# Feed-forward up projections with h's two parts side by side, 512 columns per matmul

## The chip, the cores and the metric

One core of a Trainium2 chip runs the whole program. The metric is device time in microseconds (us), the median of several executions. The engines are TensorE (PE, with its weight loads shown apart as PEld), VectorE (DVE), ScalarE (ACT), GpSimd (POOL) and SyncE (SP); the last two only issue transfers here.

## What is computed

A decoder trunk of two layers over a sequence of 256 positions, model width 1024, all in float32. Each layer is a token mixer followed by a feed-forward half; only the latter is touched:

```python
def conv_glu(h, w_up, conv_w, conv_b, w_down):
    up = causal_dwconv(h @ w_up, conv_w, conv_b)
    u, g = up[..., :D_FF], up[..., D_FF:]
    return (jax.nn.gelu(g) * u) @ w_down          # D_FF = 2816
...
h = modulate(rmsnorm(x, ffn_pre_g[l]), sh_f, sc_f)
y = conv_glu(h, ffn_w_up[l], ffn_conv_w[l], ffn_conv_b[l], ffn_w_down[l])
x = x + g_f[:, None, :] * rmsnorm(y, ffn_post_g[l])
```

The depthwise convolution has three taps over the positions. The modulation vectors (sh, sc, g) are rows of `ada_w` times a vector; the kernel works them out on VectorE, a tile of 128 x 1024 at a time, all through the layer.

## The kernel before

Matrix products run in a reduced float32 format, so each operand is split into a high part (rounded, by ScalarE) and the remainder (by VectorE), and each product is made of three matmuls: high weights times the remainder of h, low weights times the high part of h, high times high (`mm3`, line 1589). Weights stream in as blocks of 1 MB (128 partitions x 2048) through a ring of three slots: SyncE loads `raw`, ScalarE writes `w_hi` (lines 543 and 920), VectorE writes `w_lo` (lines 1033 and 1533) and so releases `raw` for the next load; TensorE frees the pair of slots when its product ends (semaphore `blk_used`).

The feed-forward half has 11 pairs. Pair i is an up product for the gate (part 0, `up_proj(2i, 0)`), one for the value (part 1, `up_proj(2i+1, 1)`) and then the down product of the pair before (`down_proj(i - 1)`). An up product makes 2 tiles of 128 features (b) x 256 positions, each a sum over 8 chunks (k) of 3 matmuls with 256 moving columns: 48 matmuls. A down product is 24 matmuls of 512 moving columns. Part 0 lies in PSUM bank 4, part 1 in bank 5, both b side by side; bank 6 takes the two `gate_rows` products near the end of the half.

Behind each up product, ScalarE writes the middle tap with its bias from PSUM to `EF` (`conv`, line 901, two instructions), VectorE adds the other two taps (`conv`, line 1510, four instructions), and its semaphore `up_c` lets TensorE write the bank again. ScalarE then applies the gelu to part 0 (line 908), VectorE multiplies the parts into `tmp` (`hidden`, line 1524), ScalarE rounds them (`hidden_hi`, line 912) and VectorE takes the remainder (`hidden_lo`, line 1528; semaphore `f_lo`), which `down_proj(i)` waits for. Every engine's order is written out by hand: the list in the ScalarE part begins at line 922, that of VectorE at line 1535, that of TensorE at line 2049, and an engine that waits holds up everything behind it.

Between these VectorE does the modulation sums: `ada_sum` (line 1026) and `ffn_sum` (line 1549) reduce one 512 KB tile in `adw`, which has two slots; when one is used up, GpSimd issues the next load into it (line 496), and the sum of that tile waits for its landing. In the head of the half VectorE does sums NT and NT+1, then the first convolution, the split of block NM+3 (pair 1's value weights), sum NT+2, the second convolution, the split of block NM+4 (the first down weights), sum NT+3, `hidden(0)` and `hidden_lo(0)`. Sum NT+2 uses the slot that sum NT leaves, NT+3 the one that NT+1 leaves.

## Time and profile before

| | before |
|---|---|
| time, median of 3 runs | 1001.82 us (1000.3 to 1004.57) |
| the profiled execution | 1004.92 us, its span 1003.3 us |
| PE busy | 974.2 us, 97% |
| PEld busy | 912.4 us, 91% |
| DVE busy | 713.8 us, 71% |
| ACT busy | 525.3 us, 52% |
| granted TensorE clock, mean | 0.979 |
| the chain that ended last | PE 94%, DVE 2%, ACT 2% |

The span reaches from the first to the last instruction of the profiled execution; its time has 1.6 us more around it. In the timeline a duration includes the tail of an instruction that overlaps the next one on the same engine, so the pace of a row of equal instructions is read from the distance between their starts. The feed-forward half of layer 0 lies at 327 to 516 us, that of layer 1 at 809 to 998 us.

### The profile page before, as it was taken

The page shows a single profiled execution, that of the slowest core. Times are in us where ns is not written, and L with a number is a line of the kernel's source. Part 1 is how long each engine was busy: PE and PEld are TensorE (multiplying, and loading weights), DVE is VectorE, ACT ScalarE, POOL GpSimd, SP SyncE. Part 2 cuts the span into 40 slices and gives each one's busy share as a digit, 9 for nine tenths or more (in the row PEclk, how much of TensorE's full clock was granted, in tenths as well). Part 3 has the DMA queues.
Part 4 walks back from the last instruction along what each step waited for, and adds up shares of the span by engine and source line. Part 5 has one row for each costly group of instructions (what it writes and reads, how often), then busy time and mean ns, then how long its engine had stood idle before and what let it go on. Part 6 is the DMA issues. An engine that isn't in the chain of part 4 may idle for free.

```text
span 1003.3 us, 17990 instructions
## 1 busy us (share of the span) xinstructions
PE 974.2 (97%) x7040; PEld 912.4 (91%) x7040; DVE 713.8 (71%) x948; ACT 525.3 (52%) x700; POOL 43.8 (4%) x85
## 2 busy tenths in 40 slices
PE   7999999999999999999989999999999999999997
PEld 7999999999987999999978999899998889999996
DVE  2579865766686888787776876666657688767675
ACT  3435857443456654545564366654344666454554
POOL 0000000000000000000000000000100000000000
PEclk7599999999999999999999999999999999999999
DMA  9876745566464777776734874556746557555541
GB/s 354 282 241 211 255 169 168 171 228 212 147 226 152 252 256 247 244 258 233 269 127 134 282 235 129 187 162 208 242 146 231 189 190 260 183 182 191 173 161 42
DMA packets 134137, 206.34 MB, mean 206 GB/s; under 512 B 6336, under 2 KB 104384, under 8 KB 133952
## 3 DMA queue, kind: packets, MB, share of 16 engines
q1 hardware_dynamic: 122416, 162.07, 49.5%
q0 software_dynamic: 11520, 41.95, 11.5%
q10 hardware_dynamic: 144, 1.51, 0.4%
q8 instruction: 42, 0.69, 0.3%
q14 instruction: 15, 0.12, 0.0%
HBM read 204.46 MB, written 1.05 MB: 205 GB/s over the span
## 4 chain that ended last, share of the span: by engine, by line
PE 94%; DVE 2%; ACT 2%; issue 1%; DMA 0%; DVEq 0%; SPq 0%; ACTq 0%
PE banks L1594 81%; PE banks L1654 2%; PE banks L1610 2%; PE banks L1880 1%; PE banks L1883 1%; PE banks L1618 1%; PE banks L1724 1%; PE banks L1706 1%; DVE x L1123 1%; PE banks L1890 1%; PE banks L1743 1%; ACT h L592 1%; PE banks L1752 0%; PE banks L1769 0%; DVE w_lo L1033 0%
## 5 line engine op out<-in xcount | busy, mean ns | idle before, releaser
L1594 PE MATMUL banks<-h_lo,w_hi 128*128 128x256 f32 x1504 | 430.4, 286 | 3.2 <-DVE h_lo L1094 3.2
L1594 PE MATMUL banks<-h_hi,w_lo 128*128 128x256 f32 x1504 | 425.5, 283 | 0.0
L1594 PE MATMUL banks<-h_hi,w_hi 128*128 128x256 f32 x1504 | 425.5, 283 | 0.0
L1594 PEld LDWEIGHTS banks<-h_lo,w_hi 128*128 128x128 f32 x1504 | 288.4, 192 | 6.7 <-DVE h_lo L1094 4.0
L1594 PEld LDWEIGHTS banks<-h_hi,w_lo 128*128 128x128 f32 x1504 | 288.5, 192 | 2.2 <-issue 1.4
L1594 PEld LDWEIGHTS banks<-h_hi,w_hi 128*128 128x128 f32 x1504 | 288.4, 192 | 0.0
L1033 DVE TENSOR_TENSOR w_lo<-raw,w_hi 128x2048 fp32r<-128x2048 f32 x82 | 187.2, 2290 | 71.6 <-ACT w_hi L543 71.5
L543 ACT ACTIVATE w_hi<-raw 128x2048 fp32r<-128x2048 f32 x82 | 156.0, 1910 | 109.6 <-PE banks L1594 99.7
L1533 DVE TENSOR_TENSOR w_lo<-raw,w_hi 128x2048 fp32r<-128x2048 f32 x56 | 128.0, 2286 | 22.7 <-ACT w_hi L920 22.6
L920 ACT ACTIVATE w_hi<-raw 128x2048 fp32r<-128x2048 f32 x56 | 107.2, 1913 | 43.9 <-PE banks L1594 43.9
L1510 DVE SCALAR_TENSOR_TENSOR EF<-banks,par,EF 128x254 f32<-128x254 f32 (+1 forms) x176 | 76.9, 478 | 51.5 <-ACT EF L901 46.0
L901 ACT ACTIVATE EF<-banks,par 128x256 f32<-128x256 f32 x88 | 44.9, 561 | 106.6 <-PE banks L1594 106.6
L1594 PE MATMUL banks<-w_hi,oa_lo 128*128 128x512 f32 x208 | 81.3, 391 | 0.0
L1594 PE MATMUL banks<-w_lo,oa_hi 128*128 128x512 f32 x208 | 81.2, 390 | 0.0
L1594 PE MATMUL banks<-w_hi,oa_hi 128*128 128x512 f32 x208 | 80.9, 389 | 0.0
L496 POOL DMA_DIRECT2D adw<-in_ada_rows x80 | 42.6, 533 | 800.9 <-DVE adw L1026 598.8
L1026 DVE SCALAR_TENSOR_TENSOR adw<-adw,cbc 128x1024 f32<-128x1024 f32 x58 | 70.3, 1220 | 3.6 <-DMA adw<-in_ada_rows 2.4
L831 ACT ACTIVATE lat<-banks 128x512 f32<-128x512 f32 x24 | 14.2, 591 | 74.7 <-PE banks L1594 74.7
L1594 PEld LDWEIGHTS banks<-w_hi,oa_hi 128*128 128x128 f32 x208 | 39.0, 188 | 8.3
L1594 PEld LDWEIGHTS banks<-w_hi,oa_lo 128*128 128x128 f32 x208 | 39.1, 188 | 7.6
L1594 PEld LDWEIGHTS banks<-w_lo,oa_hi 128*128 128x128 f32 x208 | 39.1, 188 | 7.3
L1594 PE MATMUL banks<-oa_lo,w_hi 128*128 128x256 f32 x128 | 37.2, 290 | 1.6 <-DVE EF L1459 1.6
(284 smaller groups left out, 1264.3 us busy)
## 6 DMA issues: line engine op xcount, KB each, us to landing
raw<-in_w_in SPq DMA_DIRECT2D x52, 1024.0 KB, 5.6
raw<-in_ffn_w_up SPq DMA_DIRECT2D x44, 1024.0 KB, 5.1
adw<-in_ada_rows POOLq DMA_DIRECT2D x80, 512.0 KB, 4.6
raw<-in_ffn_w_down SPq DMA_DIRECT2D x22, 1024.0 KB, 4.9
raw<-in_w_out SPq DMA_DIRECT2D x8, 1024.0 KB, 7.3
raw<-in_ret_wo SPq DMA_DIRECT2D x4, 1024.0 KB, 5.1
raw<-in_lru_wo SPq DMA_DIRECT2D x4, 1024.0 KB, 7.5
raw<-in_mla_wo SPq DMA_DIRECT2D x4, 1024.0 KB, 7.2
```

The costliest lines, as they stand in the source:

```text
L496: pool.dma_start(adw[:, slot, :], ada_v[:, bass.ds(n + ADA0, 1), :].rearrange("p a d -> p (a d)")).then_inc(adw_in[slot], 16)
L543: A_(dst, src, ACT.Copy).then_inc(hi_ready.s, 1)
L831: A_(flat2(lat, m % 2), PS[:, gate_bank(m), :], ACT.Tanh, scale=0.5).then_inc(mg_th.s, 1)
L901: a = A_(EF[:, 2 * part + b, :], PS[:, 4 + part, T * b:T * b + T], ACT.Identity, scale=par[:, l, bass.ds(i * 2 + col["tap2"] + NFF * (1 - ...
L920: A_(w_hi[:, slot, :], raw[:, slot, :], ACT.Copy).then_inc(hi_ready.s, 1)
L1026: V.scalar_tensor_tensor(adw[:, n % 2, :], adw[:, n % 2, :], 1.0, cbc[:], ALU.mult, ALU.mult, accum_out=mraw[:, n % NT:n % NT + 1]).then_i ...
L1033: V.tensor_tensor(dst, whole, hi, ALU.subtract).then_inc(lo_ready.s, 1)
L1510: v = V.scalar_tensor_tensor(EF[:, 2 * part + b, d:T], PS[:, 4 + part, T * b:T * b + T - d], par[:, l, bass.ds(i * 2 + col[f"tap{tap}"] + ...
L1533: V.tensor_tensor(w_lo[:, slot, :], raw[:, slot, :], w_hi[:, slot, :].bitcast(F32), ALU.subtract).then_inc(lo_ready.s, 1)
L1594: ins = MM(ps, lhs, rhs, start=first and n == 0, stop=last and n == 2)
L1610: ins = MM(PS[:, bank, P * i:P * i + P], x[:, c, P * kk:P * kk + P], diag[:, c, :], start=True, stop=True)
L1654: ins = MM(PS[:, (2, 7)[half], col:col + 1], ada0_buf(n)[:, P * k:P * k + P], ccol[:, 2, k:k + 1], start=k == 0, stop=k == DK - 1)
```

## The change

`h_hi` and `h_lo` become the two halves of one tensor `h_both`, so that high part and remainder of chunk k can be the moving operand of one matmul of 2 x 256 = 512 columns. An up product keeps, for each b and k, one wide matmul (high weights times both) and one narrow one (low weights times the high part, 256 columns): 16 + 16 in place of 48. The wide one fills a whole bank, so part 0 takes banks 4 and 5 and part 1 takes banks 6 and 7; columns 0 to 255 hold the sum of two products, columns 256 to 511 the third, and they have to be added. ScalarE copies the right halves to `AB` (`copy_part`), VectorE adds the left halves to them there (`add_parts`), and the convolution's instructions read `AB`. TensorE now waits for `add_parts` (`up_u`) rather than for the convolution (`up_c`). The order of splits and sums around them is changed, in the head and in the loop; of the `gate_rows` products the second goes to bank 4, and each has waits for the banks.

```diff
@@ line 214
-        h_hi = sb("h_hi", [P, DK, T], F32R)
-        h_lo = sb("h_lo", [P, DK, T], F32R)
+        h_both = sb("h_both", [P, 2, DK, T], F32R)
+        h_hi, h_lo = h_both[:, 0], h_both[:, 1]
@@ line 336
-        up_c0, up_c1, up_c = sig("up_c0", 2 * PAIRS), sig("up_c1", 2 * PAIRS), sig("up_c", 2 * PAIRS)
+        up_a, up_u = sig("up_a", 4 * PAIRS), sig("up_u", 2 * PAIRS)
+        up_c1, up_c = sig("up_c1", 2 * PAIRS), sig("up_c", 2 * PAIRS)
@@ line 410
+        def up_sum(part):
+            return AB[:, 2 * part:2 * part + 2, :]
@@ line 892
+                def copy_part(n, part, i, first=False):
+                    product_done(act, l, NM + part if first else i * 3 + (NM - 1 + part))
+                    if not first:
+                        act.wait_ge(up_c.s, up_c.at(l, i * 2 + (part - 1)))
+                    A_(up_sum(part), PS[:, 4 + 2 * part:6 + 2 * part, T:2 * T], ACT.Copy).then_inc(up_a.s, 1)
                 def conv(n, part, i, first=False):
-                    product_done(act, l, NM + part if first else i * 3 + (NM - 1 + part))
+                    act.wait_ge(up_u.s, up_u.at(l, n + 1))
                     if not first:
                         act.wait_ge(f_t.s, f_t.at(l, i))
                     for b in range(2):
-                        a = A_(EF[:, 2 * part + b, :], PS[:, 4 + part, T * b:T * b + T], ACT.Identity,
+                        a = A_(EF[:, 2 * part + b, :], up_sum(part)[:, b, :], ACT.Identity,
                                scale=par[:, l, bass.ds(i * 2 + col["tap2"] + NFF * (1 - part) + b, 1)],
                                bias=par[:, l, bass.ds(i * 2 + col["ffn_conv_b"] + NFF * (1 - part) + b, 1)])
-                    a.then_inc(up_c0.s, 1)
+                    a.then_inc(up_a.s, 1)
@@ line 919
+                copy_part(0, 0, 0, first=True)
+                split_block(l, NM + 3)
                 conv(0, 0, 0, first=True)
-                split_block(l, NM + 3)
+                copy_part(1, 1, 0, first=True)
                 gelu(0)
+                split_block(l, NM + 4)
                 conv(1, 1, 0, first=True)
-                split_block(l, NM + 4)
                 hidden_hi(0)
                 with act.Fori(1, PAIRS - 1) as i:
+                    copy_part(i * 2, 0, i)
+                    ffn_split(i, 0)
                     conv(i * 2, 0, i)
-                    ffn_split(i, 0)
+                    copy_part(i * 2 + 1, 1, i)
+                    ffn_split(i, 1)
                     gelu(i)
                     conv(i * 2 + 1, 1, i)
-                    ffn_split(i, 1)
                     ffn_split(i, 2)
                     product_done(act, l, i * 3 + (NM + 1))
                     hidden_hi(i)
                 i = PAIRS - 1
                 gate_rows(l, 1, 0, 6)
+                copy_part(i * 2, 0, i)
+                ffn_split(i, 0)
                 conv(i * 2, 0, i)
-                ffn_split(i, 0)
+                copy_part(i * 2 + 1, 1, i)
                 gelu(i)
                 conv(i * 2 + 1, 1, i)
                 hidden_hi(i, 1)
-                gate_rows(l, 1, 1, 6)
+                gate_rows(l, 1, 1, 4)
@@ line 1501
-                def conv(n, part, i, first=False):
-                    dve.wait_ge(up_c0.s, up_c0.at(l, n + 1))
+                def add_parts(n, part):
+                    dve.wait_ge(up_a.s, up_a.at(l, n * 2 + 1))
+                    V.tensor_tensor(up_sum(part), PS[:, 4 + 2 * part:6 + 2 * part, 0:T], up_sum(part), ALU.add).then_inc(up_u.s, 1)
+                def conv(n, part, i):
+                    dve.wait_ge(up_a.s, up_a.at(l, n * 2 + 2))
                     for tap in (1, 0):
                         d = 2 - tap
                         for b in range(2):
                             v = V.scalar_tensor_tensor(
-                                EF[:, 2 * part + b, d:T], PS[:, 4 + part, T * b:T * b + T - d],
+                                EF[:, 2 * part + b, d:T], up_sum(part)[:, b, 0:T - d],
@@ line 1534
-                conv(0, 0, 0, first=True)
+                add_parts(0, 0)
+                ada_sum(l, NT + 2)
                 split_block(l, NM + 3)
-                ada_sum(l, NT + 2)
-                conv(1, 1, 0, first=True)
+                conv(0, 0, 0)
+                add_parts(1, 1)
+                conv(1, 1, 0)
@@ line 1550
-                    conv(i * 2, 0, i)
-                    ffn_split(i, 0)
+                    add_parts(i * 2, 0)
                     if with_sums:
                         ffn_sum(i, 0)
+                    ffn_split(i, 0)
+                    conv(i * 2, 0, i)
+                    add_parts(i * 2 + 1, 1)
+                    if with_sums:
+                        ffn_sum(i, 1)
+                    ffn_split(i, 1)
                     conv(i * 2 + 1, 1, i)
-                    ffn_split(i, 1)
                     hidden(i)
                     ffn_split(i, 2)
                     hidden_lo(i)
-                    if with_sums:
-                        ffn_sum(i, 1)
@@ line 1568
-                conv(i * 2, 0, i)
-                ffn_split(i, 0)
+                add_parts(i * 2, 0)
                 if l + 1 < L:
                     ada_sum(l, 2 * NT - 2)
+                ffn_split(i, 0)
+                conv(i * 2, 0, i)
+                add_parts(i * 2 + 1, 1)
@@ line 2018
+                        bank, cols = PS[:, 4 + 2 * part + b, :], slice(P * b, P * b + P)
                         for k in range(DK):
-                            ins = mm3(PS[:, 4 + part, T * b:T * b + T],
-                                      (wh[:, k, P * b:P * b + P], wl[:, k, P * b:P * b + P]), h_pair(k), k == 0, k == DK - 1)
+                            if k < DK - 1:
+                                MM(bank, wh[:, k, cols], h_both[:, :, k, :], start=k == 0, stop=False)
+                            MM(bank[:, 0:T], wl[:, k, cols], h_hi[:, k, :], start=False, stop=False)
+                        ins = MM(bank, wh[:, DK - 1, cols], h_both[:, :, DK - 1, :], start=False, stop=True)
@@ line 2049
-                def up_pair(i):
-                    pe.wait_ge(up_c.s, up_c.at(l, i * 2 - 1))
+                def up_pair(i, last=False):
+                    pe.wait_ge(up_u.s, up_u.at(l, i * 2 - 1))
                     up_proj(i * 2, 0, s_g, i * 3 + (RING + NM))
-                    pe.wait_ge(up_c.s, up_c.at(l, i * 2))
+                    pe.wait_ge(up_u.s, up_u.at(l, i * 2))
+                    if last:
+                        pe.wait_ge(grow_ev.s, grow_ev.at(l, 3))
@@ line 2066
+                pe.wait_ge(up_u.s, up_u.at(l, i * 2))
                 gate_rows(l, 1, 0, 6)
-                up_pair(i)
-                pe.wait_ge(grow_ev.s, grow_ev.at(l, 3))
-                gate_rows(l, 1, 1, 6)
+                up_pair(i, last=True)
+                pe.wait_ge(up_u.s, up_u.at(l, i * 2 + 1))
+                gate_rows(l, 1, 1, 4)
```

## Rows read from the trace of the kernel before

**Rows 1.** The page: busy time of each engine, and the chain that ended last.
```profile
PE 974.2 (97%) x7040; PEld 912.4 (91%) x7040; DVE 713.8 (71%) x948; ACT 525.3 (52%) x700; POOL 43.8 (4%) x85
...
PE 94%; DVE 2%; ACT 2%; issue 1%; DMA 0%; DVEq 0%; SPq 0%; ACTq 0%
```

**Rows 2.** Timeline, TensorE, one pair (start, duration, engine, line, operation); consecutive pairs look alike.
```profile
457.52 0.28 PE L1594 MATMUL banks<-h_lo,w_hi 128*128 128x256 f32 x1
...
469.04 0.40 PE L1594 MATMUL banks<-w_hi,oa_lo 128*128 128x512 f32 x1
469.27 0.40 PE L1594 MATMUL banks<-w_lo,oa_hi 128*128 128x512 f32 x1
...
474.50 0.28 PE L1594 MATMUL banks<-h_lo,w_hi 128*128 128x256 f32 x1
```

**Rows 3.** Windows, all engines, one pair: length, then busy us (instructions) by engine.
```profile
464.86:481.84 16.98, 16.98 (x123) 16.02 (x122) 13.68 (x17) 8.73 (x10) 1.06 (x3) 1.00 0.72 246
```

**Rows 4.** Groups of instructions, VectorE: a 512-element sum that reads PSUM.
```profile
L1111 DVE TENSOR_TENSOR CD<-banks,grow 128x512 f32<-128x512 f32 x8 | 5.5, 691 | 7.8 <-ACT CD L611 7.7
```

**Rows 5.** Timeline, ScalarE: a 512-element copy out of PSUM.
```profile
494.02 0.58 ACT L659 ACTIVATE grow<-banks 128x512 f32<-128x512 f32 x1
```

**Rows 6.** Timeline, VectorE, head of layer 0's half ([idle before, and what ended it]).
```profile
333.66 1.22 DVE L1026 SCALAR_TENSOR_TENSOR adw<-adw,cbc 128x1024 f32<-128x1024 f32 x1
...
334.81 1.78 DVE L1510 SCALAR_TENSOR_TENSOR EF<-banks,par,EF 128x255 f32<-128x255 f32 x4
...
340.03 1.22 DVE L1026 SCALAR_TENSOR_TENSOR adw<-adw,cbc 128x1024 f32<-128x1024 f32 x1 [1.24 <-DMA adw<-in_ada_rows]
...
341.18 1.77 DVE L1510 SCALAR_TENSOR_TENSOR EF<-banks,par,EF 128x255 f32<-128x255 f32 x4
342.87 2.28 DVE L1033 TENSOR_TENSOR w_lo<-raw,w_hi 128x2048 fp32r<-128x2048 f32 x1
345.07 1.22 DVE L1026 SCALAR_TENSOR_TENSOR adw<-adw,cbc 128x1024 f32<-128x1024 f32 x1
...
346.21 0.69 DVE L1524 TENSOR_TENSOR tmp<-EF 128x512 f32<-128x512 f32 x1
347.60 0.69 DVE L1528 TENSOR_TENSOR oa_lo<-tmp,oa_hi 128x512 fp32r<-128x512 f32 x1 [0.70 <-ACT oa_hi L912]
```

**Rows 7.** Timeline, GpSimd: the load that the sum at 340.03 waits for.
```profile
334.48 0.53 POOL L496 DMA_DIRECT2D adw<-in_ada_rows  x1 [38.16 <-DVE adw L1026]
```

**Rows 8.** Timeline, ScalarE, head of layer 0's half.
```profile
337.24 0.63 ACT L908 ACTIVATE EF<-EF 128x512 f32<-128x512 f32 x1
338.86 1.02 ACT L901 ACTIVATE EF<-banks,par 128x256 f32<-128x256 f32 x2 [0.99 <-PE banks L1594]
339.77 1.91 ACT L543 ACTIVATE w_hi<-raw 128x2048 fp32r<-128x2048 f32 x1
```

**Rows 9.** Timeline, TensorE: start of layer 0's half, and its first down matmul.
```profile
327.05 0.39 PE L1594 MATMUL banks<-h_lo,w_hi 128*128 128x256 f32 x1 [1.45 <-DVE h_lo L1094]
...
350.18 0.40 PE L1594 MATMUL banks<-w_hi,oa_lo 128*128 128x512 f32 x1
```

**Rows 10.** Timeline, layer 1's half: its first matmul, and the sum of tile NT+2.
```profile
808.96 0.38 PE L1594 MATMUL banks<-h_lo,w_hi 128*128 128x256 f32 x1 [1.71 <-DVE h_lo L1094]
...
821.81 1.23 DVE L1026 SCALAR_TENSOR_TENSOR adw<-adw,cbc 128x1024 f32<-128x1024 f32 x1 [1.11 <-DMA adw<-in_ada_rows]
```

**Rows 11.** Timeline, end of layer 0's half: last value convolution, `hidden_lo`, last down product.
```profile
504.09 1.02 ACT L901 ACTIVATE EF<-banks,par 128x256 f32<-128x256 f32 x2 [2.25 <-PE banks L1594]
...
508.42 0.69 DVE L1528 TENSOR_TENSOR oa_lo<-tmp,oa_hi 128x512 fp32r<-128x512 f32 x1 [0.70 <-ACT oa_hi L912]
...
510.25 0.39 PE L1594 MATMUL banks<-w_hi,oa_lo 128*128 128x512 f32 x1
```

**Rows 12.** TensorE's longest idle time in the timeline, and a window after it (0.50: granted clock).
```profile
519.42 3.26 PE L1610 MATMUL banks<-diag,x 128*128 128x128 f32 x16 [3.57 <-DVE diag L1070]
...
520.03:523.44 3.41, 3.41 (x16) 3.23 (x16) 2.78 (x8) 3.03 (x7) 0.00 (x0) 0.50 0.87 290
```

## Prediction, written before the changed kernel ran

> **What bounds the kernel now.** I read the page first: TensorE is busy 97% of the span and makes up 94% of the chain that ended last [rows 1]. So TensorE's own pace and its few waits set the time; the other engines count only where they come late. Next the timeline of TensorE over one pair of the feed-forward loop, for the pace. From 457.52 to 469.04 us the 96 matmuls of the two up products take 11.52 us, 120 ns each; from 469.04 to 474.50 the 24 of the down product take 5.46, 227 ns each [rows 2]. A pair takes 16.98 us, without a gap: the windows row shows TensorE busy all of a pair, VectorE for 13.68 us of it, ScalarE for 8.73 [rows 3]. Two 256-column matmuls cost 240 ns where one of 512 costs 227: each matmul pays some 13 ns beside its columns. Last the timeline at the head and the end of the half, because there the engines wait for each other and the hand-written order decides.
>
> **TensorE's gain.** The change makes 16 wide and 16 narrow matmuls of each up product's 48. An up product should take 16 x (0.227 + 0.120) = 5.55 us instead of 5.76, a pair 16.55 instead of 16.98: 0.43 us less. With 22 pairs and 32 wide matmuls in each, 704 x 13.3 ns = 9.4 us. The trace has no alternation of wide and narrow. The nearest row is the passage from narrow to wide: the first wide matmul after the narrow ones takes 0.23 (469.04 to 469.27), against 0.227 in the mean [rows 2]. If each of them took 0.235, 5.6 us of the gain would go; a gain beyond 13.3 ns has no row behind it. I take 9.4, with 3.8 as the other end.
>
> The Trainium skill, page "TensorE: Matmul & The Clock Gate", section "Back-to-back issue gap", gives the gap between single matmuls as N / 2.4 plus 2.5 ns. By that two narrow ones cost only 2.5 ns more than a wide one, the change would save 704 x 2.5 = 1.8 us, and the sum below would come out 7.6 us longer. The rows speak against it: 120 and 227 ns, each about 13 above its columns, not 2.5.
>
> **What VectorE and ScalarE get, in the loop.** Added for each up product: a copy of 512 elements out of PSUM on ScalarE, 0.58 us [rows 5], and a 512-element sum with one PSUM operand on VectorE, 0.69 with the tail that overlaps its successor [rows 4], 0.60 net. The convolution's instructions now read SBUF. Their price there isn't in the trace; I leave it as it is. VectorE then has 13.68 + 2 x 0.60 = 14.9 us of a pair, plus some tenths of waiting, against TensorE's 16.55; ScalarE has 9.9. Both stay under it, and the weight splits and f_lo come over a microsecond ahead of their use, so in the loop these edits cost nothing. That cover is thin: had VectorE some 1.6 us more per pair, it would be the bound. Transfers: the same bytes in 2.5% less time.
>
> **What they get in the head.** Here the order matters. Now VectorE does sums NT and NT+1, the first convolution at 334.81 and a split, and then still waits 1.24 us, until 340.03, for the transfer of the tile NT+2 [rows 6]. GpSimd could issue that only at 334.48, once sum NT had released its slot [rows 7]. The change puts this sum ahead of the split of block NM+3 and ahead of both convolutions. The release of the slot and the transfers around it stay as they are, so the landing stays at 340.03, and what is queued behind the sum now waits for it. On VectorE, by the distances of starts in the same rows: sum NT+2 340.03 to 341.18; split of NM+3, 2.20, to 343.38; convolution of part 0, 1.69, to 345.07; `add_parts(1, 1)`, 0.69, to 345.76. Then ScalarE: gelu from 345.1, 0.54 net of its 0.63; split of NM+4, 1.80 net, to 347.45; its convolution, 1.02, to 348.5 [rows 8]. VectorE again: convolution 1.69, to 350.2; split of NM+4, 2.20, to 352.4; sum NT+3, 1.15, to 353.55; and from `hidden` to the end of `hidden_lo` 2.08, as from 346.21 to 347.60 + 0.69 [rows 6]: `f_lo` at 355.6.
>
> TensorE starts at 327.05 and would, at the new pace, be through three up products at 327.05 + 0.1 + 16.64 = 343.8. The fourth needs bank 6 and 7 back: `up_u` at 345.76, a stall of 2.0. It ends at 351.45, and the first down product must wait for `f_lo`: a stall of 4.25, start at 355.7. Before, that product started at 350.18 [rows 9]. So TensorE is 5.5 us later at this point, its gain of four up products already counted. Behind it VectorE carries a backlog: split of block NM+5 is ready at 359.5, needed at 361.1; the next `f_lo` at 370.5, needed at 372.1. No third stall, and from then it catches up by over a microsecond per pair. In layer 1 the half starts at 808.96 and the tile lands at 821.81, 12.85 us later, where layer 0 has 12.98 [rows 9, 10]: 5.4 us later.
>
> **The end of the half.** The last down product waits for the last `f_lo`, that now ends at 508.42 + 0.69 = 509.1, against a start at 510.25 [rows 11]. Copy and sum lie ahead of the convolution that starts at 504.09: + 0.61 + 0.72 = 1.33 us, so 510.45 and a start 0.25 late. Both `gate_rows` waits are for sums that are done some microseconds earlier; they cost nothing while VectorE keeps the loop's pace.
>
> **The clock.** TensorE's longest idle time after its start is 3.57 us, up to 519.42. After it the granted clock was 0.50 (1.2 GHz) from 520.03 to 523.44, with TensorE working again all the while [rows 12]. Idle times of 1.45 and 1.71 us left it at full speed. The new stall of 4.25 us is longer than the one that brought the fall, and dense work that needs the full clock stands behind it: 3.41 us at half speed lose 1.7 us, once in each layer. From below: nothing, if it doesn't fall.
>
> **The sum.** Layer 0: + 5.5 at the first down product, - 9 x 0.43 = - 3.85 for the nine pairs after it, + 0.25 at the end: + 1.9. Layer 1: + 1.8. Clock: + 3.4. Together + 7.1 us. The profiled execution took 1004.9 (span 1003.3 and 1.6 around it), so it would take 1012.0. It stands 3.1 above the median of the runs; against the median, 1001.8 + 7.0 = 1008.8. Where TensorE fell idle for 3.57 us between the layers, its clock may fall in one execution and not in another, which fits a spread of 4 us in the runs.
>
> **Rivals.** (1) The stall comes, the clock stays: 1005.4. For it: idle time ahead of the down product is cut by dense work on either side, where the row that fell had light work after it. (2) The gain shows whole and the head hardly stalls, because the tile lands earlier: without that wait VectorE would be through at about 351, the stall per layer 1.8 us, and the sum - 9.4 + 3.5 + 0.5, 996.4, faster. Against it: both layers show VectorE idle for this very transfer, and nothing in the change brings it forward. (3) Alternating matmuls don't keep the pace of equal ones (each wide one 0.24 or more): the gain goes, 1001.8 + 7.0 + up to 9.4 = 1012 to 1018. (4) VectorE becomes the bound of the loop from the point where its pair goes above 16.55 us, 1.6 over what I worked out: 0.5 us more in each of some 14 pairs with sums would make 1016. (5) The change doesn't do what it says, say two transfers or two matmuls where one is written: the matmul count of the page would be 7040 and not 704 less; about 1020.
>
> **How the numbers follow.** The stall with a fall of the clock in one layer or both (1007.1 to 1008.8): 0.55. (1) 0.19. (2) 0.10. (3) 0.08. (4) 0.05. (5) 0.03. Forecast 1008.8. The range leaves out (2), (5) and the far part of (3) and (4), and takes in (1) with the spread of the runs and the way towards (2): 999 to 1014. What a measurement of this kernel can tell from no change is about 0.5%, 5 us: below 996.8 is faster, above 1006.8 slower. Faster: half of (2) and a little of (1), 0.07. Slower: nearly all of the first case and of (3) to (5), and a part of (1), 0.60. Same: 0.33.
>
> **What the profile after would show.** 704 matmuls less; starts 227 and 120 ns apart in turn; 16.55 us per pair. VectorE idle for some 4.6 us at about 335 us, up to a sum released by a transfer; TensorE idle about 2 us at 344 and about 4 us at 351, released by VectorE at `AB` and at `oa_lo`; the same in layer 1. A granted clock of 0.50 near 356 us. I would be wrong if that sum started well before 340, if TensorE had no gap at 351, or if the starts stood 240 ns apart.

## The result: 1.4% slower, and the profile after

| kernel | median us (lowest to highest, runs) | profiled execution | span | PE busy |
|---|---|---|---|---|
| before | 1003.2 (1000.3 to 1005.25, 4) | 1004.9 | 1003.3 | 974.2, 7040 matmuls |
| after | 1016.71 (1012.77 to 1022.13, 4) | 1016.97 | 1015.3 | 973.4, 6336 matmuls |

The ratio of after to before, as recorded, is 1.0142, with a 95% interval of 1.0106 to 1.0178 (the quotient of the two medians is 1.0135). The predicted rise of 7.0 us had the right sign and half the size of the measured 13.5; the time lies above the range (999 to 1014). Most executions of a kernel fall into two groups some 5 us apart, by whether TensorE's first 512-column matmuls reach full pace at about 43 us or only at about 49 us. So below, stretches of two traces are compared, and totals only with their intervals.

The page of after, busy time and chain (to be read against [rows 1]):

```profile
PE 973.4 (96%) x6336; PEld 877.0 (86%) x6336; DVE 741.0 (73%) x992; ACT 551.3 (54%) x744; POOL 43.6 (4%) x85
...
PE 84%; DVE 7%; ACT 5%; issue 2%; DMA 2%; SPq 0%; DVEq 0%; POOLq 0%; ACTq 0%
```

The 704 matmuls are gone, and yet TensorE is busy as long as before, 0.8 us less. And a tenth of the chain has moved from TensorE to VectorE, ScalarE and a transfer. So there are two questions: why the gain is small, and where the waits stand.

Windows of after, two consecutive pairs of the loop (columns as in [rows 3]), and the timeline of TensorE within one:

```profile
399.85:416.57 16.72, 16.72 (x91) 14.31 (x90) 14.87 (x20) 9.85 (x11) 1.06 (x2) 1.00 0.78 254
416.57:433.29 16.72, 16.72 (x91) 14.31 (x90) 14.88 (x20) 9.86 (x11) 1.06 (x2) 1.00 0.75 251
```
```profile
399.85 0.40 PE L2053 MATMUL banks<-h_both,w_hi 128*128 128x512 f32 x1
400.09 0.28 PE L2054 MATMUL banks<-h_both,w_lo 128*128 128x256 f32 x1
400.21 0.40 PE L2053 MATMUL banks<-h_both,w_hi 128*128 128x512 f32 x1
400.44 0.28 PE L2054 MATMUL banks<-h_both,w_lo 128*128 128x256 f32 x1
```

A pair takes 16.72 us, not 16.55: 11.27 for the up products and 5.45 for the down product. A wide matmul holds TensorE for 0.23 to 0.24 us when a narrow one stands before it (399.85 to 400.09), and wide plus narrow take 11.27 / 32 = 0.352, not 0.347. VectorE is busy for 14.87 us of a pair (predicted: 14.9), ScalarE for 9.85 (9.9), and TensorE has no gap.

TensorE at the head of the half, layer 0 and then layer 1 (timeline; in brackets the idle time before, and what ended it; compare [rows 9, 10]):

```profile
326.73 0.50 PE L2053 MATMUL banks<-h_both,w_hi 128*128 128x512 f32 x1 [1.47 <-DVE h_both L1112]
...
345.28 0.50 PE L2053 MATMUL banks<-h_both,w_hi 128*128 128x512 f32 x1 [1.39 <-DVE AB L1525]
...
355.39 0.47 PE L1623 MATMUL banks<-w_hi,oa_lo 128*128 128x512 f32 x1 [4.21 <-DVE oa_lo L1551]
```
```profile
814.66 0.50 PE L2053 MATMUL banks<-h_both,w_hi 128*128 128x512 f32 x1 [1.47 <-DVE h_both L1112]
...
834.18 0.50 PE L2053 MATMUL banks<-h_both,w_hi 128*128 128x512 f32 x1 [2.34 <-DVE AB L1525]
...
844.30 0.76 PE L1623 MATMUL banks<-w_hi,oa_lo 128*128 128x512 f32 x1 [4.21 <-DVE oa_lo L1551]
```

The first down product starts 355.39 - 326.73 = 28.66 us into the half in layer 0 and 29.64 in layer 1; before it was 23.13 in both. VectorE in the same stretch of layer 0 shows the cause (compare [rows 6]):

```profile
334.49 0.69 DVE L1525 TENSOR_TENSOR AB<-banks,AB 128x512 f32<-128x512 f32 x1
...
339.48 1.23 DVE L1044 SCALAR_TENSOR_TENSOR adw<-adw,cbc 128x1024 f32<-128x1024 f32 x1 [4.31 <-DMA adw<-in_ada_rows]
...
340.63 2.29 DVE L1051 TENSOR_TENSOR w_lo<-raw,w_hi 128x2048 fp32r<-128x2048 f32 x1
342.84 1.78 DVE L1533 SCALAR_TENSOR_TENSOR EF<-AB,par,EF 128x255 f32<-128x255 f32 x4
344.54 0.68 DVE L1525 TENSOR_TENSOR AB<-banks,AB 128x512 f32<-128x512 f32 x1
348.12 1.79 DVE L1533 SCALAR_TENSOR_TENSOR EF<-AB,par,EF 128x255 f32<-128x255 f32 x4 [2.89 <-ACT EF L913]
349.82 2.29 DVE L1051 TENSOR_TENSOR w_lo<-raw,w_hi 128x2048 fp32r<-128x2048 f32 x1
```

VectorE waits 4.31 us for the tile, where it waited 1.24, with the split, a convolution and the add queued behind. Later it waits 2.89 us for ScalarE, which does gelu and a 1.8 us split before its own part of the second convolution. The clock behind the stall, windows of after in layer 0 and layer 1 (granted clock is the third number from the end; 0.56 and 0.57 are means of a stretch at 0.50 and some 0.45 us at full speed):

```profile
356.19:359.60 3.41, 3.41 (x11) 2.64 (x10) 3.41 (x5) 3.41 (x5) 0.53 (x1) 0.56 0.70 245
844.30:847.71 3.41, 3.41 (x9) 2.75 (x10) 3.41 (x4) 3.41 (x5) 0.53 (x1) 0.57 0.75 308
```

And the end of layer 0's half, TensorE and ScalarE (compare [rows 11, 12]):

```profile
515.38 0.47 PE L1623 MATMUL banks<-w_hi,oa_lo 128*128 128x512 f32 x1 [0.39 <-DVE oa_lo L1551]
...
525.36 2.85 PE L1639 MATMUL banks<-diag,x 128*128 128x128 f32 x16 [4.26 <-DVE diag L1088]
```
```profile
508.68 0.60 ACT L905 ACTIVATE AB<-banks 128x512 f32<-128x512 f32 x1 [2.25 <-PE banks L2055]
509.51 0.63 ACT L920 ACTIVATE EF<-EF 128x512 f32<-128x512 f32 x1 [0.24 <-DVE EF L1533]
510.12 1.10 ACT L913 ACTIVATE EF<-AB,par 128x256 f32<-128x256 f32 x2
513.87 0.63 ACT L924 ACTIVATE oa_hi<-tmp 128x512 fp32r<-128x512 f32 x1 [2.66 <-DVE tmp L1547]
...
518.23 0.57 ACT L616 ACTIVATE CD<-banks 128x512 f32<-128x512 f32 x1
```

The same two steps of ScalarE in the kernel before, `hidden_hi` and the first `CD`:

```profile
507.76 0.63 ACT L912 ACTIVATE oa_hi<-tmp 128x512 fp32r<-128x512 f32 x1 [2.65 <-DVE tmp L1524]
...
512.10 0.57 ACT L611 ACTIVATE CD<-banks 128x512 f32<-128x512 f32 x1
```

TensorE's idle time between the layers grew from 3.57 to 4.26 us. Put together, by the differences of such starts:

| term, us against before | predicted | measured |
|---|---|---|
| first down product, layer 0 / layer 1 | +5.5 / +5.4 | +5.53 / +6.51 |
| next pair, with the clock's fall | +1.27 / +1.27 | +1.45 / +1.24 |
| eight further pairs | -3.44 / -3.44 | -2.07 / -2.07 |
| last pair's down products to the next layer / the end | +0.25 / +0.25 | +1.35 / +0.62 |
| all else | 0 | -0.56 |
| sum | 7.06 | 12.0 |

### The profile page after: what moved, and what is told of

It reads as the page before. It is cut to its first block, busy times and chain, and to the rows that moved or that the text cites. A ratio compares the mean times of both kernels' runs of the same rounds, so it can differ in the third digit from the quotient of the medians.

```text
span 1015.3 us, 16784 instructions
## 1 busy us (share of the span) xinstructions
PE 973.4 (96%) x6336; PEld 877.0 (86%) x6336; DVE 741.0 (73%) x992; ACT 551.3 (54%) x744; POOL 43.6 (4%) x85
## 4 chain that ended last, share of the span: by engine, by line
PE 84%; DVE 7%; ACT 5%; issue 2%; DMA 2%; SPq 0%; DVEq 0%; POOLq 0%; ACTq 0%
PE banks L1623 53%; PE banks L2053 11%; PE banks L2054 6%; PE banks L1683 3%; DVE w_lo L1051 2%; PE banks L2055 2%; PE banks L1639 1%; DVE EF L1533 1%; ACT w_hi L548 1%; DMA adw<-in_ada_rows 1%; PE banks L1909 1%; PE banks L1912 1%; DVE adw L1044 1%; DMA raw<-in_ada_rows 1%; PE banks L1753 1%
## 5 line engine op out<-in xcount | busy, mean ns | idle before, releaser
L1623 PE MATMUL banks<-h_both,w_hi 128*128 128x256 f32 x1600 | 298.8, 286 | 0.0
L1623 PEld LDWEIGHTS banks<-h_both,w_hi 128*128 128x128 f32 x1600 | 252.1, 192 | 2.1 <-issue 1.2
L2053 PE MATMUL banks<-h_both,w_hi 128*128 128x512 f32 x616 | 221.5, 398 | 6.7 <-DVE AB L1525 3.7
L1623 PE MATMUL banks<-h_both,w_lo 128*128 128x256 f32 x800 | 226.3, 283 | 0.0
L2054 PE MATMUL banks<-h_both,w_lo 128*128 128x256 f32 x704 | 183.3, 281 | 0.0
L1623 PEld LDWEIGHTS banks<-h_both,w_lo 128*128 128x128 f32 x800 | 153.4, 192 | 1.6 <-issue 1.4
L2053 PEld LDWEIGHTS banks<-h_both,w_hi 128*128 128x128 f32 x616 | 115.9, 188 | 32.8 <-DVE AB L1525 4.4
L2054 PEld LDWEIGHTS banks<-h_both,w_lo 128*128 128x128 f32 x704 | 132.9, 189 | 7.9
L1533 DVE SCALAR_TENSOR_TENSOR EF<-AB,par,EF 128x254 f32<-128x254 f32 (+1 forms) x176 | 77.1, 480 | 13.6 <-ACT EF L913 8.1
L905 ACT ACTIVATE AB<-banks 128x512 f32<-128x512 f32 x44 | 26.4, 599 | 95.7 <-PE banks L2055 95.6
L1623 PEld LDWEIGHTS banks<-w_hi,oa_lo 128*128 128x128 f32 x208 | 39.9, 192 | 18.1 <-issue 10.6
L913 ACT ACTIVATE EF<-AB,par 128x256 f32<-128x256 f32 x88 | 47.9, 593 | 1.4 <-DVE AB L1525 0.8
```

The source lines that it names most:

```text
L913: a = A_(EF[:, 2 * part + b, :], up_sum(part)[:, b, :], ACT.Identity, scale=par[:, l, bass.ds(i * 2 + col["tap2"] + NFF * (1 - part) + b, 1)],
L1533: v = V.scalar_tensor_tensor(EF[:, 2 * part + b, d:T], up_sum(part)[:, b, 0:T - d], par[:, l, bass.ds(i * 2 + col[f"tap{tap}"] + NFF * (1 ...
L1623: ins = MM(ps, lhs, rhs, start=first and n == 0, stop=last and n == 2)
L2053: MM(bank, wh[:, k, cols], h_both[:, :, k, :], start=k == 0, stop=False)
L2054: MM(bank[:, 0:T], wl[:, k, cols], h_hi[:, k, :], start=False, stop=False)
```

## Experiments

In each result "first down" is the time from the half's first up matmul to its first down matmul, "end" the time in layer 0 from the last pair's first down matmul to the next layer's first matmul (`diag`), and "pair" the period in the loop, all in us. Before: 23.13, 14.72, 16.98. After: 28.66 (layer 1: 29.64), 16.07, 16.72. Numbers in square brackets behind a ratio are its 95% interval.

### The pace of TensorE

**e2_grouped**: the change, with the seven wide matmuls of a tile together and the eight narrow ones after them.

```diff
-                        for k in range(DK):
-                            if k < DK - 1:
-                                MM(bank, wh[:, k, cols], h_both[:, :, k, :], start=k == 0, stop=False)
+                        for k in range(DK - 1):
+                            MM(bank, wh[:, k, cols], h_both[:, :, k, :], start=k == 0, stop=False)
+                        for k in range(DK):
                             MM(bank[:, 0:T], wl[:, k, cols], h_hi[:, k, :], start=False, stop=False)
```

> The changed kernel with the same matmuls in another order: in each tile 7 wide ones, then the 8 narrow ones, then the last wide one. Theory (a wide matmul behind a narrow one takes 235 ns, behind a wide one 227): the two up products of a pair take 11.1 us in place of 11.27, the time falls by 3 to 4 us. Rival (the wide one pays for its moving operand in two runs of 256, wherever it stands): starts stay 235 ns apart among the wide ones too, 11.27 us a pair, and the time stays.

Timeline of TensorE in the loop, e2_grouped:

```profile
430.68 1.75 PE L2052 MATMUL banks<-h_both,w_hi 128*128 128x512 f32 x7
432.26 1.12 PE L2054 MATMUL banks<-h_both,w_lo 128*128 128x256 f32 x8
433.21 0.40 PE L2055 MATMUL banks<-h_both,w_hi 128*128 128x512 f32 x1
433.45 1.77 PE L2052 MATMUL banks<-h_both,w_hi 128*128 128x512 f32 x7
435.06 1.11 PE L2054 MATMUL banks<-h_both,w_lo 128*128 128x256 f32 x8
```

In the group behind a down product seven wide ones take 1.58 us, 0.226 each. The wide one that follows a narrow one takes 0.24 (433.21 to 433.45), and the seven behind it still 1.61 (433.45 to 435.06), 0.230 each. The up products take 11.15 us, a pair 16.61. So it is the passage from narrow to wide that costs, some 7 to 10 ns in the first wide one and something in the next few, and not that the wide operand lies in two pieces: in the first group it does so too. The kernel before shows the same where the operand is in one piece: the first five matmuls of its down product take 1.16 us (469.04 to 470.20), 0.232 each, against 0.227 further on. The time of the whole, 1016.2 against 1004.65, ratio 1.0111 [1.0073, 1.0149], can't be told from the change's; the expected 3 to 4 us are 0.5 in layer 0 and 2.2 in layer 1 by the traces, from the half's start to the last pair's down products. Of the 2.2, 1.55 come from the pair behind the head (16.67 us in place of 18.22, see the last section). First down was at 29.20 and 29.80, later than in after although the matmuls are faster, because the tile landed later (see step three below).

**e11_narrow**: e6_head_grouped (below), with 24 of a pair's 32 wide matmuls taken apart again into two narrow ones. All else stays, copies and adds too.

```diff
-                        for k in range(DK - 1):
-                            MM(bank, wh[:, k, cols], h_both[:, :, k, :], start=k == 0, stop=False)
+                        MM(bank, wh[:, 0, cols], h_both[:, :, 0, :], start=True, stop=False)
+                        for k in range(1, DK - 1):
+                            MM(bank[:, T:2 * T], wh[:, k, cols], h_lo[:, k, :], start=False, stop=False)
+                            MM(bank[:, 0:T], wh[:, k, cols], h_hi[:, k, :], start=False, stop=False)
```

> e6 with the wide matmuls taken apart again, but for the first and last of each tile: each of the other 24 of an up product's... of a pair's 32 becomes two of 256 columns with the same weights; copies, sums and all orders stay. Theory (the wide form saves one matmul's fixed 13 ns each, less what a passage from narrow to wide costs): a pair takes 16.95 to 17.0 us in place of 16.61, 7 to 8 us more than e6. Rival (the pace is set by VectorE or by the weight loads, not by the count of matmuls): a pair stays below 16.8 us.

A pair took 16.85 us, not 16.95 to 17.0: the estimate was 0.1 too high, but above the rival's 16.8, so the count of matmuls does set the pace. The 24 are worth 16.85 - 16.61 = 0.24 us, 10 ns each. All 32, grouped, are worth 0.37 (16.98 before, 16.61 in e6), 8 us in 22 pairs; as the change orders them, 0.26 us, 5.7 in all. The total, 999.48 against 1004.66, ratio 0.9979 [0.9956, 1.0001], has an interval that overlaps e6's, so here only the traces tell the two apart.

### The order in the head

**e1_sum_later**: the change, with the sum of tile NT+2 moved back, behind the split and the first convolution.

```diff
                 add_parts(0, 0)
-                ada_sum(l, NT + 2)
                 split_block(l, NM + 3)
                 conv(0, 0, 0)
+                ada_sum(l, NT + 2)
                 add_parts(1, 1)
```

> The changed kernel with one thing moved: in the head of each half VectorE does sum NT+2 (the one that waits for its transfer) behind the split of NM+3 and the first convolution, not ahead of them. Theory (the order of the head makes the stalls and, through TensorE's 4.2 us idle time, the fall of its clock): the first down product starts some 24.0 us after the half's first matmul, in place of 28.7 and 29.6; the granted clock of 0.50 at 356 and 844 us is gone; together 4.7 + 5.6 + 3.4 = 13.7 us less than the changed kernel, so about the time of the kernel before (ratio 1.000 to 1.003). Rival (VectorE's and ScalarE's added work is what costs, wherever it stands): the idle time only moves to later pairs, and under 4 us come back (ratio above 1.010).

1002.3 against 1004.65, ratio 0.9984 [0.996, 1.0008], as the theory had it. One line in another place is worth 1.6% by the ratios; by the traces, from the half's start to the last pair's down products, 6.1 us in layer 0 (182.56 to 176.45) and 6.9 in layer 1. TensorE and VectorE of e1_sum_later in layer 0:

```profile
328.19 0.50 PE L2053 MATMUL banks<-h_both,w_hi 128*128 128x512 f32 x1 [1.46 <-DVE h_both L1112]
...
352.34 0.47 PE L1623 MATMUL banks<-w_hi,oa_lo 128*128 128x512 f32 x1 [1.41 <-DVE oa_lo L1551]
```
```profile
341.08 1.22 DVE L1044 SCALAR_TENSOR_TENSOR adw<-adw,cbc 128x1024 f32<-128x1024 f32 x1 [0.55 <-DMA adw<-in_ada_rows]
...
342.23 0.69 DVE L1525 TENSOR_TENSOR AB<-banks,AB 128x512 f32<-128x512 f32 x1
345.06 1.79 DVE L1533 SCALAR_TENSOR_TENSOR EF<-AB,par,EF 128x255 f32<-128x255 f32 x4 [2.15 <-ACT EF L913]
```

The wait for the transfer is 0.55 us instead of 4.31, first down is at 24.15 and 24.18, TensorE's stalls are 1.41 us instead of 1.39 and 4.21, and the clock's fall is gone in both layers: the next down product follows 16.84 us later, not 18.43. What is left is VectorE's wait of 2.15 us for ScalarE.

**e8_before_sum_first**: the kernel before, with nothing but that sum moved forward. The reverse test.

```diff
                 conv(0, 0, 0, first=True)
-                split_block(l, NM + 3)
                 ada_sum(l, NT + 2)
+                split_block(l, NM + 3)
                 conv(1, 1, 0, first=True)
```

> The kernel before with the one move in VectorE's list that the change makes in the head: sum NT+2 ahead of the split of NM+3. Theory (the wait for the transfer does its harm only together with the longer chain: copy, sum, and ScalarE's gelu and split ahead of its second convolution): f_lo at 23.4 us after the half's start, against 23.1 when it is needed: a stall of 0.3 to 0.4 us per layer, no fall of the clock, ratio 1.000 to 1.002. Rival (the moved sum alone makes the stalls): the first down product starts 26 us or more after the half's start, ratio 1.006 or more.

1006.51 against 1001.6, ratio 1.0028 [1.0004, 1.0051]; first down 24.10 and 24.31, so 1.0 and 1.2 us later. I had expected 0.3 to 0.4 and the rival 3; the theory was nearer, but its size was a third of the measured one. VectorE waits 3.52 us for the transfer here too, but only 1 us of it reaches TensorE. So the moved sum does most of its harm together with the longer chain that the change puts behind it: undone in the change it gives 4.5 and 5.5 us at the first down product, alone it costs 1.0 and 1.2.

**e4_both**: e1 and e2 together.

> The order of the head of e1 and the order of matmuls of e2 together. Theory: 13.7 and 3.9 us less than the changed kernel, the sum of the two, about 999 us (ratio 0.995 to 0.998). Rival (they meet the same limit): no better than the better of the two.

1000.83 against 1004.65, ratio 0.9982 [0.9957, 1.0007], hardly better than e1's 0.9984: of the 3.9 us expected from the grouping, the traces show 2. First down stays at 24.11, with 1.50 us idle before it: four up products on TensorE got faster, but the chain on VectorE and ScalarE sets that start. Only the later pairs (16.61) show the gain, 1 us per layer.

**e6_head_grouped**: e4_both, with ScalarE's part of the second convolution ahead of its split, and VectorE's sums behind the work that TensorE waits for.

```diff
                 gelu(0)
-                split_block(l, NM + 4)
                 conv(1, 1, 0, first=True)
+                split_block(l, NM + 4)
                 hidden_hi(0)
...
                 conv(0, 0, 0)
-                ada_sum(l, NT + 2)
                 add_parts(1, 1)
                 conv(1, 1, 0)
+                ada_sum(l, NT + 2)
                 split_block(l, NM + 4)
-                ada_sum(l, NT + 3)
                 hidden(0)
                 hidden_lo(0)
+                ada_sum(l, NT + 3)
```

> On top of e4: in the head ScalarE does its second convolution ahead of the split of NM+4, and VectorE does both sums (NT+2, NT+3) behind the convolutions, NT+3 behind hidden_lo(0). By the rows of e4, f_lo comes some 22.3 us after the half's start instead of 24.1. Theory (the rest of the stall is the order of the head too): the 1.5 us of idle time ahead of each first down product are gone, it starts 22.5 to 22.7 us after the half's start; 3 us less than e4, ratio 0.993 to 0.997. Rival (the chain copy, sum, convolution is too long for any order there): 1 us or more of the stall stays.

1000.2 against 1001.6, ratio 0.996 [0.994, 0.998]. First down 22.45 and 22.48, with no idle time before it (timeline of TensorE, the last up matmul and the first down one):

```profile
343.80 0.40 PE L2055 MATMUL banks<-h_both,w_hi 128*128 128x512 f32 x1
344.03 0.40 PE L1623 MATMUL banks<-w_hi,oa_lo 128*128 128x512 f32 x1
```

So the copy, the add and the longer chain can be hidden whole in the head; the order of the lists decides.

### The clock

**e3_filled_stall**: the change, with 16 matmuls on constants (`keep_going`) ahead of the first down product, where TensorE stands idle for 4.2 us.

```diff
                     up_pair(i)
+                    if first:
+                        keep_going(0, 16)
                     for c in range(TC):
```

> The changed kernel with 16 idle matmuls of 256 columns (ident times constants into bank 0, 3.7 us, overwritten afterwards) ahead of the first down product's wait, where TensorE stands idle for 4.2 us. Nothing else moves, and the down product can't start earlier. Theory (the clock's fall is a cost of its own, 1.7 us per layer): no granted clock of 0.50 behind the stall, and 3.4 us less than the changed kernel. Rival (the fall is hidden, since VectorE is behind there anyway): the fall is gone from the trace and the time stays within 1 us.

The fill was too large: the profile shows each as two matmuls, 32 in all, and they held TensorE from 347.12 to 353.83, 6.7 us, past the end of the wait. First down was at 31.73 in layer 0, 3.1 us later than in after, and at 31.28 in layer 1, 1.6 later. 1018.56 against 1004.65, ratio 1.0157 [1.0101, 1.0214]. The fall was gone (the next down product 16.95 us later), but the total says nothing on its price. Hence the next.

**e5_filled_8**: the same with 8.

> e3 again with 8 idle matmuls in place of 16: e3's trace shows that one of them takes 0.44 us, so that 16 took 6.7 us and held the down product up by 3 us more than the stall. 8 take 3.5 us of the 4.2 us of idle time. Theory (the clock's fall behind the stall is a cost of its own): first down product 28.7 to 29.6 us after the half's start as in the changed kernel, no granted clock of 0.50 behind it, from the first to the second down product 16.8 us in place of 18.4, 3.4 us less in all. Rival (the fall is hidden behind VectorE's backlog): the fall is gone and the second down product starts as late as in the changed kernel.

```profile
350.67 3.62 PE L1653 MATMUL banks<-cst 128*128 128x256 f32 x16
355.05 0.47 PE L1623 MATMUL banks<-w_hi,oa_lo 128*128 128x512 f32 x1 [0.77 <-DVE oa_lo L1551]
```

In layer 0 the wait stays where it was (first down 28.58), TensorE stands idle for 0.77 us of it, and the next down product follows after 16.82 us, where the change took 18.43; in layer 1 it is 16.80 and 18.22. So the fall costs 1.4 to 1.6 us per layer. 1012.93 against 1001.6, ratio 1.01 [1.0063, 1.0137]: against the change's 1.0142 some 4 us, with intervals that overlap. By the traces 3.0 us are the clock's, and 0.8 come from layer 1's first down at 28.82 in place of 29.64, because the tile landed earlier there (step three below). What is left of the loss is the wait itself.

### The end of the half

**e7_last_old**: e6, with the last value product in its old form (narrow matmuls, one bank, convolution from PSUM), so without copy and add. VectorE's part of the edit:

```diff
                 conv(i * 2, 0, i)
-                add_parts(i * 2 + 1, 1)
-                conv(i * 2 + 1, 1, i)
+                dve.sem_inc(up_u.s, 1)
+                conv(i * 2 + 1, 1, i, bank=6)
                 hidden(i)
```

> On top of e6: the last value product of each half (part 1 of pair 10) in the old form: 48 matmuls of 256 columns into bank 6, no copy, no sum, the convolution reads PSUM. Theory (at the end of a half copy and sum lie on the path, through the last down product's wait and ScalarE's list behind hidden_hi): TensorE's 0.4 us of idle time ahead of the last down product is gone, that between the layers is 3.6 us again instead of 4.26; 0.2 us more for the 16 matmuls; 1 us less per half, 2 in all. Rival (the end is bound by other work): idle time between the layers stays at 4.2 us.

995.13 against 1001.6, ratio 0.9941 [0.9913, 0.9969]; end 15.76, where I had expected about 15.1. The 0.4 us ahead of the last down product are gone, but the idle time between the layers stayed at 4.28 us, as the rival had it. ScalarE shows why: its last gelu waits for VectorE's first convolution.

```profile
495.63 0.63 ACT L920 ACTIVATE EF<-EF 128x512 f32<-128x512 f32 x1 [3.08 <-DVE EF L1538]
```

**e9_last_old_ordered**: e7, with this convolution ahead of the split and the sum. **e10_end_ordered**: e6 with that order, the last product wide. ScalarE's convolution and split change places likewise.

```diff
                 add_parts(i * 2, 0)
+                conv(i * 2, 0, i)
+                ffn_split(i, 0)
                 if l + 1 < L:
                     ada_sum(l, 2 * NT - 2)
-                ffn_split(i, 0)
-                conv(i * 2, 0, i)
```

> On top of e7: in the last pair VectorE and ScalarE do the convolution of part 0 ahead of the last weight split (and VectorE's sum), as in the kernel before. e7's trace shows the gelu waiting for that convolution until 0.9 us after the last value product's end, so that taking copy and sum away saved 0.4 us and not 1.3. Theory (the order of the last pair hides what copy and sum cost): TensorE's idle time between the layers is 3.6 us in place of 4.28, from the last pair's first down matmul to the next layer's first matmul 14.7 to 14.9 us in place of 15.8; some 1 us less per half than e7, ratio 0.990 to 0.994. Rival (that stretch is bound elsewhere): it stays at 15.8 us.

> On top of e6, the order of e9 alone: last value product in the wide form, with copy and sum. Theory: copy and sum then cost their own 1.3 us on ScalarE's list at the end of a half, of which the better order gives back 0.15: idle time between the layers 4.1 to 4.2 us, 0.1 to 0.3 us per half less than e6. Rival (only the order was wrong): idle time 3.6 us, 1 us less per half.

e9: 994.31 against 1004.66, ratio 0.9927 [0.9896, 0.9958], end 15.35 (expected 14.7 to 14.9), with 4.19 us idle between the layers (expected 3.6). e10: 997.17, ratio 0.9954 [0.9929, 0.998], end 17.40, longer than in e6, with 1.73 us idle ahead of the last down product. VectorE of e10_end_ordered:

```profile
496.02 1.22 DVE L1044 SCALAR_TENSOR_TENSOR adw<-adw,cbc 128x1024 f32<-128x1024 f32 x1
...
497.17 0.69 DVE L1525 TENSOR_TENSOR AB<-banks,AB 128x512 f32<-128x512 f32 x1
499.02 1.79 DVE L1533 SCALAR_TENSOR_TENSOR EF<-AB,par,EF 128x255 f32<-128x255 f32 x4 [1.17 <-ACT EF L913]
```

The sum, which nobody at this point waits for, now stands right ahead of the add, on which the rest of the chain waits.

**e12_end_sums_last** and **e13_last_old_sums_last**: e10 and e9 with this sum behind the last `hidden_lo`.

```diff
                 ffn_split(i, 0)
-                if l + 1 < L:
-                    ada_sum(l, 2 * NT - 2)
...
                 hidden_lo(i, 1)
                 if l + 1 < L:
+                    ada_sum(l, 2 * NT - 2)
                     ada_sum(l, 2 * NT - 1)
```

> On top of e10 (wide last value product, with copy and sum): the modulation sum of the last pair goes behind hidden_lo. e10's trace has VectorE busy with that sum until 497.17 us, when the last add_parts could have started at 495.7. Theory (copy and sum cost 1.3 us at the end of a half even in the best order): from the last pair's first down matmul to the next layer's first matmul 16.1 to 16.3 us (e10 17.4, kernel before 14.72), idle time between the layers 4.2 us. Rival (the end was a matter of order alone): 14.7 to 15.0 us.

> On top of e9 (last value product in the old form): the modulation sum of the last pair behind hidden_lo. e9's convolution on VectorE starts at 496.82, 0.85 us after ScalarE's part of it is done. Theory (with the old form and this order nothing of the change is left at the end of a half): the same stretch takes 14.5 to 14.8 us as in the kernel before (e9 15.35), idle time 3.5 to 3.7 us; 0.5 to 0.8 us less than e9 in all; ratio 0.990 to 0.994. Rival: it stays above 15.2 us.

e12: 996.06 against 1004.69, ratio 0.9945 [0.9921, 0.9969], end 16.26. e13: 996.85 against 1004.69, ratio 0.9929 [0.9901, 0.9957], end 14.70, the kernel before's 14.72. Both ends are as expected. TensorE's first matmul of the next layer, e12 and then e13:

```profile
512.09 3.78 PE L1638 MATMUL banks<-diag,x 128*128 128x128 f32 x16 [4.29 <-DVE diag L1088]
```
```profile
515.98 3.26 PE L1643 MATMUL banks<-diag,x 128*128 128x128 f32 x16 [3.57 <-DVE diag L1093]
```

The two differ in the last value product alone, and by 1.56 us in the end. That is what copy and add cost in this order at the end of layer 0; after layer 1, to the end of the span, it is 0.8 us (17.5 and 16.6). e12's order is no better than the change's own (16.26 against 16.07): VectorE's add, free to start at 495.8 when ScalarE's copy is done, starts at 496.14 behind the last weight split. An order with that split behind the add was not tried, so 1.56 is not shown to be the least. e9 and e13 are faster than both kernels: 0.7% against before, and 2% against the change by the quotient of two ratios. They can't be told from each other.

## Why the prediction was wrong

**Right.** The sum ahead of the split as the cause in the head; both stalls and their releasers (the first 2.0 us predicted, 1.39 and 2.34 measured; the second 4.25 predicted, 4.21 measured in both layers); first down in layer 0 (28.65 predicted, 28.66 measured, and the last digits are luck: the sum started 0.23 us earlier than in the row used, the chain behind it took 0.24 longer); the fall of the clock behind it and its price (1.7 predicted, 1.4 to 1.6 by e5); VectorE's and ScalarE's load in the loop; the price of the copy (0.60) and of the add (0.69); that the convolution costs the same from SBUF (VectorE's mean is 480 ns, before 479; ScalarE's 593 against 561, which nothing in the loop feels). e1 shows the cause in the head: with the one line back, stall and fall are gone and 1.6% with them. It spoke against a rival that the prediction had not named, that copy and add alone make the head so long. They and the new order of ScalarE's list make it 1 us longer (24.15 against 23.13). e8 adds that the early sum alone makes it 1.0 to 1.2 longer; it takes both for 5.5.

**Wrong, step one: the term for TensorE's gain, about 3 us of the 5 that were missing.** I priced a wide matmul at 0.227, the mean of equal ones in a row. The row that I had named as nearest, the first wide one after narrow ones, showed 0.23, and I took 0.235 only as the far end. It is the value, and only the narrow one behind it is a little shorter (0.117 in place of 0.120): 0.352 for wide plus narrow, so 0.26 us gained per pair and not 0.43: 5.7 us in 22 pairs, and not 9.4. In the four up products at the head the waits cover this; in the nine pairs after them it shows, 2 x 9 x 0.17 = 3.1 us. The table has it as 2 x 1.37 in the eight pairs and 0.2 in the next pair of layer 0. e2 showed that the passage is what costs. The Trainium skill, page "TensorE: Matmul & The Clock Gate", section "Back-to-back issue gap", with its 2.5 ns beside N / 2.4, would make wide plus narrow 0.325 us and make one wide one worth 2.5 ns against two narrow ones, an estimate worked out from its figure for single matmuls. The traces don't agree: 0.352, with 8 ns for each wide one in after and 10 in e11. But its direction, that merging matmuls saves less than my 13 ns each, was right, and I had put it aside because equal matmuls in a row spoke against it. That the page of after has TensorE busy only 0.8 us less comes in part from the two falls of the clock, which take back 3.0 of the 5.7 us; the rest wasn't taken apart.

**Wrong, step two: the end of the half, 1.35 us and not 0.25.** I set the 1.33 us of copy and add (0.58 and 0.69 in the rows; the rest had no row) against the slack of the last `f_lo` ahead of the last down product, and found 0.25 left. `hidden_hi`, and with it `f_lo`, came 1.52 us later against the pair's first down matmul (4.58 in place of 3.06), and the last down product 0.54 later, 0.39 of it idle time beyond the tail of the matmul before. What I had left out is that the same convolution has a second consumer, ScalarE's list behind `hidden_hi`: the copy of `grow`, table load, split, and then the first `CD`, which before began at 512.10 without any idle time. It had no slack. `hidden_hi` to `CD` takes 4.36 us after and 4.34 before, so the delay arrived whole at `CD`, and 1.35 of it at the next layer's first matmul, 0.7 us of that as more idle time between the layers. e12 against e13, which differ in nothing but the last value product, shows that the copy and the add do it: 1.56 us. After layer 1 the last stretch took 0.62 us more, not 0.25, nearly all of it the later last down product. Together 1.5 us that the sum lacked.

**Wrong, step three: layer 1's landing, 1.1 us (+6.51, not +5.4).** I took layer 1's head as a copy of layer 0's, since before it was one to 0.13 us. After, the sum waited for its tile until 13.73 us into the half there, against 12.75 in layer 0. GpSimd had issued the load 6.3 us earlier, in layer 0 5.3:

```profile
828.39 1.22 DVE L1044 SCALAR_TENSOR_TENSOR adw<-adw,cbc 128x1024 f32<-128x1024 f32 x1 [5.29 <-DMA adw<-in_ada_rows]
```

The other traces show this to be scatter of the transfer. Start of the sum of tile NT+2, in us from the half's first up matmul, where it waits for the tile; GpSimd issues the load at 7.43 or 7.44 in every one:

| | sum starts, layer 0 / 1 | first down, layer 0 / 1 |
|---|---|---|
| before | 12.98 / 12.85 | 23.13 / 23.13 |
| after | 12.75 / 13.73 | 28.66 / 29.64 |
| e2_grouped | 13.29 / 13.91 | 29.20 / 29.80 |
| e5_filled_8 | 12.68 / 12.92 | 28.58 / 28.82 |
| e1_sum_later | 12.89 / 13.90 | 24.15 / 24.18 |
| e8_before_sum_first | 13.05 / 13.27 | 24.10 / 24.31 |

With the sum ahead of the split, as in after, e2 and e5, first down follows 15.9 us behind it each time; the mechanism was right, and only the landing was another draw. In e1, with the sum moved back, a landing 1 us later moves first down by 0.03. So the change did not only lengthen the head, it also tied it to a time that scatters by 1.2 us. Why one load takes longer than another isn't settled. When one transfer decides a chain, its scatter belongs in the range.

**The remaining rivals.** "The clock stays" fell: in after it fell in both layers. "The tile lands earlier" fell: VectorE still waits for it, 4.31 and 5.29 us. "VectorE becomes the bound" fell: 14.87 of 16.72 us. "It doesn't do what it says" fell: 6336 = 7040 - 704. "Alternating matmuls don't keep the pace" (1012 to 1018) was the one closest to the time, though its price was half of its far end. The three misses all pointed to slower, the third by chance, and my range had room for only one of them.

By the table the sum lacked 4.9 us: 2.9 by the pace, 1.1 by the landing and 1.5 by the ends, less 0.6 in stretches that no term was for. The stretches account for the profile's 12.0 us. The medians differ by 13.5, and the interval of the ratio reaches from 10.6 to 17.9, so the two agree.

## What to carry to other kernels

Saving matmuls by widening them pays most while the wide ones follow each other (here 0.37 us a pair grouped, 0.26 alternating): group equal sizes, and price a mixed order by the passage between sizes, not by the mean of either. When a change lengthens a chain, look for every reader of its end, not only for the engine on the critical path; the one whose list already runs without idle time has no cover to give. And a step that waits for a transfer belongs behind everything in its engine's list that TensorE is waiting for: here one such line, with the change's longer chain, its wait and the clock's fall behind it, cost 6 to 7 us a layer (about 1 us where the chain was short), where the wide matmuls gain 2.9.

## What the runs showed of the hardware, unexpected

- A 512-column matmul holds TensorE 0.226 to 0.227 us in a row of its size and 0.23 to 0.24 behind one of 256 columns; the next three or four are still a little slower (0.232 in the mean of five in before, 0.230 in the mean of seven in e2). The 256-column one behind a wide one doesn't suffer (0.117 in after, 0.12 in a row).
- The granted clock was 0.50 for 3.41 us around the end of the 4.21 us of idle time in both layers of after, and for 3.41 or 6.83 us around the restart between the layers in all fifteen traces, where the idle time was 3.57 to 4.29 us. In layer 0 of e2_grouped 2.03 us of idle time brought no fall; in layer 1 2.68 us came with one from 834.9 to 841.8 us. There it hardly cost anything (first down 0.6 us later than in layer 0, as the tile's landing was, and the next pair in 16.67 us), because the wait for `f_lo` that follows shrank from 4.25 to 1.42 us: dense work at half speed ran in time that would have been idle.

```profile
835.59 3.36 PE L2052 MATMUL banks<-h_both,w_hi 128*128 128x512 f32 x7 [2.68 <-DVE AB L1525]
...
845.68 0.47 PE L1623 MATMUL banks<-w_hi,oa_lo 128*128 128x512 f32 x1 [1.42 <-DVE oa_lo L1551]
```

- In seven of the fifteen traces (e3, e5 to e9 and e12) the granted clock fell once more, for 3.41 us at 599 to 611 us, in a part that no edit touches and with no idle time of TensorE in the microseconds before. What brought it is open; it is one more reason to compare stretches and not totals.
- A 256-column matmul on plain float32 constants shows as two in the profile and takes 0.42 us of TensorE (6.71 us for 16 in e3; the 3.62 for 8 in e5 include the last one's tail). Such fillers have to be sized by a measured row.
